# GLA steps elsewhere in VectorE's queue, its first units in other quarters, and mLSTM heads in two parts

## What is computed

```
layer 1: h = rmsnorm(x)
  y_a = sigmoid(o) * norm(mLSTM(silu(conv(q, k)), v, gates))    4 heads of 256
  y_b = three groups of dilated window attention                8 heads of 64
  x = x + (sigmoid(ga) * (y_a @ w_a) + sigmoid(gb) * (y_b @ w_b)) @ w_out
  x = x + (silu(h2 @ w_gate) * (h2 @ w_up)) @ w_down;  x = rmsnorm(x, norm_final)
layer 2: h = rmsnorm(x, pre)
  o_gla = norm(GLA(q, k, v, decays)) * silu(r)                  4 heads, 128 and 256
  o_nsa = compressed + selected + windowed attention            8 heads of 64
  x = x + rmsnorm((sigmoid(mg) * (o_gla @ w_g) + sigmoid(mn) * (o_nsa @ w_n)) @ w_out)
  x = x + rmsnorm(FFN(rmsnorm(x)))
```

## Time and profile before

| | |
|---|---|
| median of 3 runs | 2049.53 us |
| profiled execution | 2049.81 us |
| its span | 2048.0 us |
| TensorE busy, instructions | 1971.6 us (96%), 9642 |
| VectorE busy | 1053.1 us (51%) |
| ScalarE busy | 635.0 us (31%) |
| GpSimd busy | 285.9 us (14%) |
| mean granted TensorE clock | 0.981 |
| HBM over the span | 83 GB/s |

### The profile page before, as it was taken

The page is one execution under the profiler, slowest core; times in us unless marked ns, Lnnn a source line. Parts: engine busy times, 40 slices in busy tenths (PEclk is TensorE's granted clock), DMA queues, the critical chain, the costliest instruction groups (busy, mean ns, idle before and its releaser), DMA issues.

```text
span 2048.0 us, 23700 instructions
## 1 busy us (share of the span) xinstructions
PE 1971.6 (96%) x9642; PEld 1596.9 (78%) x9642; DVE 1053.1 (51%) x1507; ACT 635.0 (31%) x1053; POOL 285.9 (14%) x190
## 2 busy tenths in 40 slices
PE   6999999999999999999998988999999999999997
PEld 5777788888888888888886777777777878888885
DVE  6666644344555644344344655546676644344344
ACT  4333322223333432222233322224344333222221
POOL 3122220011111111010021000111111131011012
PEclk9999999999999999999998899999999999999998
DMA  4222223232211323232322211221110322323322
GB/s 158 65 82 72 83 83 113 92 94 72 83 62 49 118 93 102 93 102 94 97 79 76 72 52 62 83 93 63 56 62 34 118 62 93 103 93 98 98 83 71
DMA packets 52444, 171.87 MB, mean 84 GB/s; under 512 B 5879, under 2 KB 9279, under 8 KB 52336
## 3 DMA queue, kind: packets, MB, share of 16 engines
q1 hardware_dynamic: 51616, 169.21, 25.9%
q10 hardware_dynamic: 720, 1.15, 0.2%
HBM read 168.12 MB, written 2.21 MB: 83 GB/s over the span
## 4 chain that ended last, share of the span: by engine, by line
PE 86%; DVE 9%; ACT 3%; issue 1%; POOL 1%; DMA 0%; DVEq 0%; POOLq 0%; ACTq 0%
PE PS L947 26%; PE PS L949 25%; PE PS L948 25%; PE PS L1245 1%; DVE WL L1576 1%; PE PS L1060 1%; PE PS L1047 1%; PE PS L1223 1%; PE PS L1267 1%; PE PS L1012 1%; PE PS L1084 1%; PE PS L1093 1%; PE PS L1107 1%; ACT WH L1310 1%; DVE AR L1610 1%
## 5 line engine op out<-in xcount | busy, mean ns | idle before, releaser
L947 PE MATMUL PS<-HH,WH 128*128 128x512 f32 x1368 | 549.3, 402 | 15.5 <-DVE WL L1576 12.2
L949 PE MATMUL PS<-HH,WL 128*128 128x512 f32 x1368 | 536.6, 392 | 0.0
L948 PE MATMUL PS<-HL,WH 128*128 128x512 f32 x1368 | 535.7, 392 | 0.0
L947 PE MATMUL PS<-AH,WH 128*128 128x512 f32 x1096 | 438.6, 400 | 11.5 <-DVE WL L1576 5.3
L1576 DVE TENSOR_TENSOR WL<-RAW,WH 128x1024 fp32r<-128x1024 f32 (+2 forms) x257 | 325.1, 1265 | 218.0 <-ACT WH L1310 216.3
L1310 ACT ACTIVATE WH<-RAW 128x1024 fp32r<-128x1024 f32 (+2 forms) x320 | 325.7, 1018 | 357.1 <-PE PS L949 357.0
L949 PE MATMUL PS<-AH,WL 128*128 128x512 f32 x1096 | 431.7, 394 | 0.0
L948 PE MATMUL PS<-AL,WH 128*128 128x512 f32 x1096 | 431.6, 394 | 0.0
L947 PEld LDWEIGHTS PS<-HH,WH 128*128 128x128 f32 x1368 | 258.8, 189 | 76.2 <-DVE WL L1576 10.9
L949 PEld LDWEIGHTS PS<-HH,WL 128*128 128x128 f32 x1368 | 258.5, 189 | 55.6
L948 PEld LDWEIGHTS PS<-HL,WH 128*128 128x128 f32 x1368 | 259.0, 189 | 53.5 <-issue 1.0
(11 more groups left out here) (241 smaller groups left out, 1432.1 us busy)
## 6 DMA issues: line engine op xcount, KB each, us to landing
RAW<-wst SPq DMA_DIRECT2D x288, 512.0 KB, 3.4
RAW<-wst SPq DMA_DIRECT2D x16, 384.0 KB, 3.0
RAW<-wst SPq DMA_DIRECT2D x16, 256.0 KB, 2.5
XT<-xT SPq DMA_DIRECT2D x3, 512.0 KB, 7.9
AR<-scr SPq DMA_DIRECT2D x16, 64.0 KB, 4.3
AR<-scr SPq DMA_DIRECT2D x8, 128.0 KB, 4.7
AR<-w SPq DMA_DIRECT2D x2, 512.0 KB, 4.1
out<-XT SPq DMA_DIRECT2D x4, 256.0 KB, 2.0
```

Source lines behind the costliest of these rows:

```text
L947: T.matmul(out, wh, XH[:, k, :], start=k == 0, stop=False)
L948: T.matmul(out, wh, XL[:, k, :], start=False, stop=False)
L949: m = T.matmul(out, wl, XH[:, k, :], start=False, stop=k == nk - 1)
```

## The change

It only moves work, but for three things: the second norm's root is taken from `mean2 + EPS * (mean1 + EPS)` in one VectorE step, so that both roots come from one POOL power over 8 columns; the divisor of a mLSTM head is worked out for its four blocks at once; the diagonal mask is added for four blocks at once. It gives `vm` units a second buffer, and the weights of a head are made in place in `WT`. `OB` is bank 5 now and the turn banks are 6 and 7.

```diff
-        self.hold(5 + self.turn % 2, *key)
+        self.hold(6 + self.turn % 2, *key)
...
+def lead_two(e, a):
+    b, c, d = a + 1, a + 2, a + 3
+    ahead(e, a)
+    for i in (a, b, c):
+        e.sum_bank("sum", i)
+    e.products(a, range(0, 2))
+    e.products(b, range(0, 2))
+    flush(e)
+    for k in (2, 4):
+        e.products(a, range(k, k + 2))
+        e.products(b, range(k, k + 2))
+    ahead(e, b)
+    for k in (0, 2, 4):
+        e.products(c, range(k, k + 2))
+    for i in (a, b):
+        e.products(i, range(6, 8))
...
+    e.two_folds()
+    ahead(e, c)
+    e.products(c, range(6, 8))
+    quarter(e, d, 0)
+    quarter(e, d, 1)
...
+    e.two_spreads()
+    evict(e, a)
+    evict(e, b)
+    quarter(e, d, 2)
+    flush_all(e)
+    quarter(e, d, 3)
+    evict(e, c)
+    evict(e, d)
...
-        fill = Fill(e, range(at, at + n), 15)
+        fill = Fill(e, range(at, at + n), 1)
         at += n
+        mlstm_scores(e, h)
+        fill.quarters(4)
+        e.weights(h)
+        fill.quarters(12)
+        for t in range(4):
+            e.hold((*SB, OB)[t], "numer", h, t)
+        e.numerators(h)
+        fill.quarters(6)
+        e.normed(h)
+        e.turns_apart = h < 3
+        fill.quarters(10 if h < 3 else 6)
+        if h == 3:
+            mlstm_scores(e, 4)
+        fill.drain(h == 3)
...
+def mlstm_scores(e, h):
+    if h < 4:
         e.turn_bank("max", h)
         e.spread_max(h)
...
+    if h:
+        e.turn_bank("hm", h - 1, 0)
+        e.gated(h - 1, 0)
+    if h < 4:
...
+        e.scores(h, (0,))
+    if h:
+        e.turn_bank("hm", h - 1, 1)
+        e.gated(h - 1, 1)
+    if h < 4:
+        e.scores(h, (1, 2, 3))
+    flush(e)
+    if h:
+        e.split_ya(h - 1)
...
-    for n, j in GLA_FIRST[2:]:
+    for n, j in GLA_FIRST[3:]:
         unit(e, unit_of(n, j))
-    e.later.append(("final", 0, 1))
+        if n == "gk":
+            e.decay(1, 0)
+            e.later.append(("decay", 1, 1))
     e.ring = [0, 1]
     for h in range(4):
         gla_turned(e, h)
-        if h < 3:
-            e.decay(h + 1, 0)
-            e.later.append(("decay", h + 1, 1))
         units(e, GLA_UNITS[h][0])
...
         e.gla_outs(h)
         if h == 3:
             e.compress_load()
+        units(e, GLA_UNITS[h][1][:1])
+        e.gla_scaled(h)
+        if h < 2:
+            e.decay(h + 2, 0)
+            e.later.append(("decay", h + 2, 1))
+        if h == 0:
+            e.later.append(("final", 0, 1))
+        if h == 3:
             e.compress_blocks(0)
-            e.compress_blocks(1)
-        units(e, GLA_UNITS[h][1])
+        units(e, GLA_UNITS[h][1][1:])
     gla_turned(e, 4)
     last = GLA_UNITS[3][2]
-    units(e, last[:2])
+    units(e, last[:1])
+    e.compress_blocks(1)
+    units(e, last[1:2])
...
     if h:
-        e.split_yg(h - 1)
+        e.later.append(("yg", h - 1, 1))
...
-                elif name == "down" and k0 == 16:
-                    act.wait_ge(*at("free", "sum", i))
-                    s.scaled_hi("h3", AH, j, XT[:, j, :], GG[:, j:j + 1])
-                    s.square("n3", j, XT[:, j, :])
-                    s.square("n4", j, XT[:, j, :], col("final_g", j))
+                elif name == "down":
+                    act.wait_ge(*at("free", "sum", i))
+                    s.scaled_hi("h3", AH, j, XT[:, j, :], GG[:, j:j + 1])
+                    s.square("n3", j, XT[:, j, :])
+                    s.square("n4", j, XT[:, j, :], col("final_g", j))
...
             def two_folds(s):
-                c1, c2, c12 = RC[:, 0:4], RC[:, 4:8], RC[:, 8:12]
                 s.fold("n3")
                 dve.wait_ge(*at("folded", "n4"))
-                dve.wait_ge(*at("root", "n3"))
-                t = V.tensor_tensor(c2, PS[:, s.bank["fold", "n4"], 0:4], c1, ALU.mult)
+                dve.wait_ge(*at("free", "fold", "n3"))
+                t = V.scalar_tensor_tensor(out=RC[:, 4:8], in0=RC[:, 0:4], scalar=EPS,
+                                           in1=PS[:, s.bank["fold", "n4"], 0:4], op0=ALU.mult, op1=ALU.add)
```

More of the change, by code:

```diff
@@ L262, in flush @@
             e.later.append(("decay", 0, 1))
+        elif what == "yg":
+            e.split_yg(i)
         elif what == "final":
@@ L312, in lead @@
     b, c = a + 1, a + 2
+    if norm == "n3":
+        return lead_two(e, a)
     for q in range(4):
@@ L1046, in scores, with numerators @@
                     pe.wait_ge(*at("mq", unit_of("km", 2 * h + c)))
[L1047 to L1053 removed]
+                for t_ in blocks:
+                    x, a = SCORES[t_]
+                    b, n = s.bank["scores", h, x], 512 - 128 * t_
+                    s.free("scores", h, x)
+                    for c in (0, 1):
+                        t = T.matmul(PS[:, b, a:a + n], k[:, c * 512 + t_ * 128:c * 512 + t_ * 128 + 128],
+                                     q[:, c * 512 + t_ * 128:c * 512 + 512], start=c == 0, stop=c == 1)
+                    t.then_inc(*pe_done["mlstm"].next("scored", h, t_))
+            def numerators(s, h):
+                v = heads_of(hv[h % 2])
                 pe.wait_ge(*at("ones"))
@@ L1742, in after @@
                     V.tensor_scalar(x, x, 0.5, 0.5, ALU.mult, ALU.add).then_inc(*dve_done["attn"].next("gate", i))
+                elif name == "down":
+                    dve.wait_ge(*at("gg"))
+                    dve.wait_ge(*at("free", "sum", i))
+                    s.scaled_lo("h3", AH, AL, j, XT[:, j, :], GG[:, j:j + 1])
                 elif name in ("pb", "pn"):
@@ new lines, in weights @@
+            def weights(s, h):
+                for t_ in range(4):
+                    x, a = SCORES[t_]
+                    n, o = 512 - 128 * t_, wo[t_]
+                    dve.wait_ge(*at("scored", h, 3 if x == 1 else t_))
+                    dve.wait_ge(*at("exp", h, t_))
+                    t = V.scalar_tensor_tensor(out=WT[:, o:o + n], in0=PS[:, s.bank["scores", h, x], a:a + n],
+                                               scalar=1.0 / 64.0, in1=WT[:, o:o + n], op0=ALU.mult, op1=ALU.mult)
+                    t.then_inc(*dve_done["mlstm"].next("weights", h, t_))
+                    if t_ != 1:
+                        dve_done["mlstm"].named("free", "scores", h, x)
@@ new lines, in normed, with gated @@
+            def normed(s, h):
+                dve.wait_ge(*at("rs_m", h))
+                for i in range(4):
+                    x = hm[:, i * 256:(i + 1) * 256]
+                    V.tensor_scalar(x, x, stat[:, 32 + 2 * i:33 + 2 * i], rs_m[:, i:i + 1], ALU.subtract,
+                                    ALU.mult).then_inc(*dve_done["mlstm"].next("normed", h, i))
+            def gated(s, h, j):
+                dve.wait_ge(*at("hm_turned", h, j))
+                dve.wait_ge(*at("gate", unit_of("om", 2 * h + j)))
+                t = V.scalar_tensor_tensor(out=ya[j], in0=PS[:, s.bank["hm", h, j], :], scalar=col("mnorm", 2 * h + j),
+                                           in1=so[:, j * 512:(j + 1) * 512], op0=ALU.mult, op1=ALU.mult)
+                t.then_inc(*dve_done["mlstm"].next("free", "hm", h, j))
@@ L2189, in split, with after @@
                 t.then_inc(*weight_lo_pool.next("lo", i))
+            def after(s, i, p):
+                name, j, k0, nk = UNITS[i]
+                if name == "down":
+                    s.add_up("n3", j)
+                    s.add_up("n4", j)
             def fold(s, norm):
```

240 lines of the change are left out of this document (94 added, 146 removed).

## The result

The changed kernel takes 2025.72 us (median of 4 runs, 2022.21 to 2026.46) against 2049.91 us (2048.44 to 2050.86) on the same chip: ratio 0.9882, 95% interval 0.987 to 0.9895. Its profiled execution took 2025.35 us, span 2023.6, against 2049.81 and 2048.0 before. So 24.5 us went, 2.9 more than the 21.6 of the sum.

The account below looks back on a forecast made before the run. The prediction took TensorE to bound the kernel wherever it is fed, so VectorE moves pay only where TensorE waits. From 2049.8 us, -8.2 -1.35 -3.2 -1.0 -1.6 -6.2 = -21.6 gave 2028.2 us, range 2012 to 2042.

Parts of the forecast that it names:

- the ring of the down units: Last down units: VectorE and ScalarE steps set a 5.7 us pace against 4.0 of products; cutting it gives -8.2 us.
- Two norms: Fold and spread: wait of 2.0 us before small2's transposes is covered by six products moved ahead, -1.35 us.
- gk0 to gv3: GLA around head 0's scores: 7.6 us of waits and clock go, 4.4 of new waits come, -3.2 us.
- (a): New TensorE wait for gv2's lower weights, behind decay 0 and one more gate step: 2.0 us, no clock loss booked.
- (b): New TensorE wait at gk0's transposes while VectorE works through its queue: 1.3 us.
- (c): New TensorE wait of head 0's updates for gk0's copy: 1.1 us.
- Head 1: GLA: wait 5.2 and clock 2.0 go; 3.1 to 3.3 at `on` half 1, with clock loss 6.2, come: -1.0 us.
- Head 2: GLA: wait 5.2 and clock 1.4 go; 3.0 at gk2's transposes and clock loss 2.0 come: -1.6 us.
- Head 3: GLA compression split in two, each bank read first: wait 4.5 and clock 1.7 go, -6.2 us.
- the backlog that never reaches TensorE: Rival: VectorE's pieces lie closer, so new waits of 4.4, 6.2 and 5.0 us vanish: 2012.6 us; chance 0.15.
- the clock behind every smaller wait: Rival: clock falls 2.0 us behind three waits near gk0 and three mLSTM head starts: +12, 2040 us; chance 0.15.
- The slower rival, solid mLSTM pieces: Rival: eight solid pieces of mLSTM scores and numerators cost 3.5 us of clock each: +28, 2056 us; chance 0.05.

Follow-up runs that it names:

- experiment 1: Kernel before the change, GpSimd's two adds of squares in the last down units made to wait for the next VectorE weight split: 2044.30 against 2050.09 us.
- experiment 7: Changed kernel with head 0's log-sigmoid and scan on VectorE ahead of a memset and the three other log-sigmoids: 2023.64 us.
- experiment 4: Changed kernel with each GLA head's scaling back right behind the output matmuls: 2021.26 us.
- Experiment 10: Changed kernel with scaling back, VectorE's decay 0 work spread out, and final norms and four compression steps laid in VectorE's idle time: 2008.98 us.
- experiment 2: Changed kernel with halves, squares and GpSimd's sums of the last down units back in evict: 2035.01 us.
- experiments 5: Changed kernel with all eight compression steps in one piece again, still behind nq0's eviction: 2025.81 us.
- 11: Changed kernel with head 3's scaling and all eight compression steps ahead of nq0's unit and eviction, as before the change; one execution: 2027.38 us.
- experiment 6: Changed kernel with the blocks of scores and numerators of each mLSTM head set apart again by products: 2023.42 us.
- 9: Changed kernel with decay 0's scan first, its other steps one flush later, the memset moved, log-sigmoids 2 and 3 behind decay 1's scan: 2020.73 us.
- experiment 8: Changed kernel with decay 3 behind unit gk2 instead of behind gr3: 2020.99 us.

## Why the prediction was right, and where its terms were off

The forecast was 2028.2 us in a range of 2012 to 2042; 2025.7 was measured. Every stretch named went the way it was said to. But the ring of the down units was long mainly for a reason that the record named only as a point against the change, the mLSTM part was booked at nothing and gave 1.4 us, and several terms are near their size because errors in them cancel. Two of its sums are also off by their own parts, without weight: 4.1 - 2.7 is 1.4 at gk0's transposes, not 1.3, and 13.1 - 9.2 - 0.9 is 3.0 at `on` half 1, not 3.1 to 3.3.

- **Down units, -8.2: -9.2.** Waits and pitch as forecast: no wait for lower weights is left, and the residual adds lie 4.09 us apart (1065.74, 1069.83). The record counted the waits and one window of clock; a wait also drains the pipeline. Before, products ran from 1075.65 and, after a wait of 1.02 us, from 1081.02: 5.37 us for 18 products, where 4.08 + 1.02 is 5.10. The record put ScalarE's order first and the turn-taking as a remark worth at most 2.4 us against the change; experiment 1 shows that removing the turns at the split alone gives 7.6. The change does the same as a side effect: the adds come behind the next split, and meet the lower half instead. In two of the eight units the lower half pays for it (1.80 us, the last row here), unseen by TensorE; in the others it starts ahead of the adds or meets none:

```profile
1070.83 0.96 DVE L1648 TENSOR_TENSOR WL<-RAW,WH 128x768 fp32r<-128x768 f32 x1 [0.32 <-ACT WH L1376]
1071.71 0.74 DVE L1633 SCALAR_TENSOR_TENSOR AL<-XT,COL,AH 128x512 fp32r<-128x512 f32 x1
1073.90 0.69 DVE L1732 TENSOR_TENSOR XT<-XT,PS 128x512 f32<-128x512 f32 x1 [1.45 <-PE PS L1010]
1075.13 1.22 DVE L1648 TENSOR_TENSOR WL<-RAW,WH 128x1024 fp32r<-128x1024 f32 x1 [0.54 <-ACT WH L1376]
1076.27 1.80 DVE L1633 SCALAR_TENSOR_TENSOR AL<-XT,COL,AH 128x512 fp32r<-128x512 f32 x1
```

- **Two norms, -1.35: -1.45.** The wait of 2.0 is 0.6. That the sizes meet is luck: with the same instructions this stretch was 3.2 us shorter in five other executions and 1.6 in two (experiment 7).
- **gk0 to gv3, -3.2: +2.0 - 5.7 = -3.6.** (a) gv2's weights: 2.0 forecast, 1.8 measured, which is luck in part, since the same wait is 3.4 or 5.0 us in executions where TensorE came there earlier (experiment 7); and 1.6 of clock behind it (12 products in 4.57 us from 1139.72 against 3.01 elsewhere), for which nothing was booked. (b) 1.3 at gk0's transposes: none, because TensorE came there 1.6 us later for its low clock; in experiment 4, where the clock stayed full behind the same wait, 1.1 us stand there (the second of its 2.7). (c) 1.1 at the updates: 0.5.
- **Head 1, -1.0: -2.4.** Experiment 10 has no wait left in this stretch and takes 36.41 us for it. What went is right (43.58 - 36.41 = 7.2; 5.2 of wait and 2.0 for clock and drain). What is new is 4.8 for 6.2. The wait at `on` half 1 is 2.4 for 3.1 to 3.3, in the place forecast. The wait for gk1's copy is 1.4 for 0.9, and it stands one step earlier, at `on` half 0, whose turn bank those tokens had; the profile names L2045, but that step began 0.08 us before the copy was done:

```profile
1180.53 0.63 PE L1250 MATMUL PS<-C,AR 128*128 128x128 f32 x4 [1.42 <-DVE AR L2045]
```

```profile
1179.70 0.68 DVE L1835 COPY AR<-PS 128x512 f32<-128x512 f32 x1
1180.30 0.16 DVE L2045 COPY AR<-AR 128x8 f32<-128x8 f32 x1
```

  A wait of 0.6 us for an eviction (line 1676) was not seen. The step that failed is the clock loss of 2.0: the window behind the 2.4 us reads 1.00. It failed in this execution, not in all: behind the same wait 12 products took 3.01 us here and in six other kernels, 3.96 us in experiment 2, which has the same instructions there, and 4.59 us in experiment 4.
- **Head 2, -1.6: -1.8.** Wait 3.2 for 3.0, clock and drain 1.7 for 2.0. What the record did not ask is whether the scaling had to be in that sum at all; experiment 4 says no.
- **Head 3, -6.2: -4.9.** The 4.5 us and their clock went. The step "each bank is read first" missed that the second half now ends behind the matmuls that need it: a wait of 1.1 us. And not the cut in two, on which the step rested, but the place behind nq0's eviction did it (experiments 5 and 11).
- **mLSTM heads, 0: -1.4.** Clock 1.00, as taken. "A gain of some tenths from fewer turns" was named and not booked; by experiment 6 it is some 0.7 us, and the other half of the 1.4 has no cause shown.

Of the rivals, the backlog that never reaches TensorE and the clock behind every smaller wait are each half true: of the seven new waits in GLA five were forecast within 0.8 us (1.8, 0.5, 1.4, 2.4, 3.2), two were not seen (0.6, 1.1), one that was forecast stayed away, and the clock fell behind two. The slower rival, solid mLSTM pieces, is refuted by experiment 6 and by the clock of 1.00 from 100 to 300 us. The sum of waits in GLA, 11.0 us, was forecast as 11.4 (2.0, 1.3, 1.1, 0.9, 3.1 and 3.0); the two that were not seen make up for those that came out smaller.

## What to carry over

Before a step is moved off the path of a wait, ask what its idle time there cost: VectorE's 5.15 us ahead of the scaling cost nothing, and moving it away put 1.66 us where they counted. Look for idle time of the engine itself behind a round trip (here 2.24 us behind each of two scans) and lay work there that nobody waits for. Where a step of VectorE starts while GpSimd adds, here one of 0.75 us took 1.80; order such steps so that the one with slack is held, with an explicit wait if need be.

## What the runs showed of the hardware

- A split of 128x768 took 0.96 us with GpSimd idle and 2.03 to 2.04 us when GpSimd's adds had begun before it; the lower half of 128x512 went from 0.75 to 1.78 and 1.80 us. The hold moves to whichever of these instructions starts second, and it goes both ways: an add of GpSimd that started 0.23 us behind a lower half took 1.66 us instead of 1.29. It lasts for the one instruction under way, not for the pair of adds: the lower half that started 0.03 us behind the first add (1076.24, 1.29 us) was done at 1078.07, while the second add (1077.48) took 1.75 us. So the two engines ran in turns. The Trainium skill (GPSIMD Engine Reference, Key points) says that they contend where VectorE reads two inputs from SBUF; the trace agrees, and its size here is a wait for the other's instruction to end.
- TensorE's clock is not a function of the program alone. From the fold to the log-sigmoid matmuls, with the same instructions of TensorE, four kernels took 17.2 us, five 14.0 and two (9 and 10) 15.6, with the granted clock of the fold's window from 0.69 to 1.00; behind waits of almost the same length and work (1.81 and 1.79 us at gv2) the next 12 products took 4.57 us in the changed kernel and 3.01 us in experiment 4. What decides it no run here shows. The Trainium skill (TensorE: Matmul & The Clock Gate, The HAM clock gate) says that one and the same kernel shows different numbers of slow matmuls at its start from run to run. These executions show the like in the middle of a kernel. The 3.2 us between them are about as large as the spread of the runs of one kernel (2022.21 to 2026.46), and experiment 8's four runs took 2018.18, 2018.44, 2023.55 and 2023.62 us at mean granted clocks of 0.990, 0.989, 0.986 and 0.986; so a difference of 3 us between medians of four runs says little by itself, and the ledger of a stretch says more.
- A low clock costs nothing where another engine's chain ends the stretch: 25.71 us to gv2's weights at either level.
